# Splitting the third weight chunk of the two gated up projections earlier, and taking the last stage's mean of squares after two contraction tiles

## What is computed

```python
def rmsnorm(x, g):
    xf = x.astype(jnp.float32)
    y = xf * lax.rsqrt(jnp.mean(xf * xf, axis=-1, keepdims=True) + EPS)
    return (y * g.astype(jnp.float32)).astype(x.dtype)

def swiglu(x, w_gate, w_up, w_down):
    return (jax.nn.silu(x @ w_gate) * (x @ w_up)) @ w_down

h = h + 0.5 * swiglu(rmsnorm(h, ffn1_norm[l]), ffn1_w_gate[l], ffn1_w_up[l], ffn1_w_down[l])
...
h = h + 0.5 * swiglu(rmsnorm(h, ffn2_norm[l]), ffn2_w_gate[l], ffn2_w_up[l], ffn2_w_down[l])
```

## Time and profile before

| | |
|---|---|
| median of 3 runs | 2094.03 us |
| lowest, highest | 2090.93, 2095.31 us |
| the profiled execution's own time | 2093.15 us |
| its span, first to last instruction | 2091.3 us |
| PE busy | 1983.7 us (95%) |
| DVE busy | 1005.7 us (48%) |
| ACT busy | 727.0 us (35%) |
| mean granted TensorE clock | 0.983 |
| DMA, mean over the span | 93 GB/s |

### The profile page before, as it was taken

One profiled execution on the slowest core, in us unless ns is written; L12 is line 12 of the kernel. 1 busy time (PEld: TensorE's weight loads), 2 busy tenths in 40 slices (PEclk: granted clock), 3 DMA queues, 4 the chain that ended last, 5 costly groups with the idle time before them and its releaser, 6 DMA issues.

```text
span 2091.3 us, 26797 instructions
## 1 busy us (share of the span) xinstructions
PE 1983.7 (95%) x10909; PEld 1671.3 (80%) x10909; DVE 1005.7 (48%) x1364; ACT 727.0 (35%) x972; POOL 23.8 (1%) x45
## 2 busy tenths in 40 slices
PE   5899999997999999979999999899999999999997
PEld 2787887873888888769999999687888878888885
DVE  7688753436455542264443322667323454444323
ACT  2454444324445532152222212455333332222111
POOL 0100000000000000000000000000000000000000
PEclk9999999998999999999999999999999999999999
DMA  6644212220222222212222222211112222222221
GB/s 269 215 158 134 99 61 102 102 99 20 81 97 83 100 83 97 102 39 82 100 80 94 72 95 92 73 61 42 61 61 81 102 81 99 100 100 74 97 90 61
DMA packets 34847, 195.45 MB, mean 93 GB/s; under 512 B 3680, under 2 KB 3696, under 8 KB 19552
## 3 DMA queue, kind: packets, MB, share of 16 engines
q1 hardware_dynamic: 29008, 173.55, 23.6%
q0 software_dynamic: 5776, 21.02, 3.1%
HBM read 192.46 MB, written 2.10 MB: 93 GB/s over the span
## 4 chain that ended last, share of the span: by engine, by line
PE 88%; DVE 8%; ACT 2%; issue 1%; DMA 1%; SPq 0%; DVEq 0%; ACTq 0%
PE PS L600 86%; DVE W_lo L1625 2%; DVE INV L1669 1%; DMA A_low<-in_wada 1%; PE PS L756 1%; ACT W_hi L1184 1%; DVE N L1674 1%; DVE A_high L2103 1%; DMA ring<-in_wada 0%; DVE ring L2103 0%; DVE RS L1646 0%; DVE PT_lo L1707 0%; DVE stats L1692 0%; DVE X L2135 0%; DVE stats L1856 0%
## 5 line engine op out<-in xcount | busy, mean ns | idle before, releaser
L600 PE MATMUL PS<-H_hi,W_hi 128*128 128x512 f32 (+1 forms) x1976 | 632.2, 354 | 48.8 <-DVE H_lo L1657 19.4
L600 PE MATMUL PS<-H_hi,W_lo 128*128 128x512 f32 (+1 forms) x1976 | 632.9, 354 | 0.0
L600 PE MATMUL PS<-H_lo,W_hi 128*128 128x512 f32 (+1 forms) x1976 | 632.0, 354 | 0.0
L1625 DVE TENSOR_TENSOR W_lo<-W_raw,W_hi 128x2048 fp32r<-128x2048 f32 (+2 forms) x170 | 352.9, 2076 | 311.6 <-ACT W_hi L1184 311.0
L600 PEld LDWEIGHTS PS<-H_hi,W_hi 128*128 128x128 f32 x1976 | 350.0, 191 | 106.6 <-issue 42.8
L1184 ACT ACTIVATE W_hi<-W_raw 128x2048 fp32r<-128x2048 f32 (+2 forms) x170 | 295.6, 1739 | 325.4 <-PE PS L600 324.6
L600 PEld LDWEIGHTS PS<-H_lo,W_hi 128*128 128x128 f32 x1976 | 349.3, 191 | 50.6 <-issue 0.2
L600 PEld LDWEIGHTS PS<-H_hi,W_lo 128*128 128x128 f32 x1976 | 349.1, 191 | 49.9 <-issue 0.2
L600 PE MATMUL PS<-G_hi,W_lo 128*128 128x512 f32 (+1 forms) x704 | 210.2, 339 | 0.0
L600 PE MATMUL PS<-G_hi,W_hi 128*128 128x512 f32 (+1 forms) x704 | 209.6, 338 | 0.0
L600 PE MATMUL PS<-G_lo,W_hi 128*128 128x512 f32 (+1 forms) x704 | 209.3, 338 | 0.0
(11 more groups left out here) (246 smaller groups left out, 2045.2 us busy)
## 6 DMA issues: line engine op xcount, KB each, us to landing
W_raw<-in_wts SPq DMA_DIRECT2D x119, 1024.0 KB, 4.8
W_raw<-in_wdown SPq DMA_DIRECT2D x48, 704.0 KB, 4.1
ring<-in_wada POOLq DMA_DIRECT2D x32, 512.0 KB, 3.8
A_high<-in_wada SPq DMA_DIRECT2D x6, 1024.0 KB, 18.0
A_low<-in_wada SPq DMA_DIRECT2D x2, 1024.0 KB, 10.5
X<-in_xT SPq DMA_DIRECT2D x2, 1024.0 KB, 10.0
X<-in_xT POOLq DMA_DIRECT2D x1, 2048.0 KB, 8.8
out<-N SPq DMA_DIRECT2D x8, 256.0 KB, 2.1
```

The lines of the kernel that those rows point to most:

```text
L600: return nc.tensor.matmul(*a, **kw)
L1625: vector.tensor_tensor(W_lo[:, c.odd, 0:size], W_raw[:, c.odd, 0:size], W_hi[:, c.odd, 0:size].bitcast(FP32), ALU.subtract).then_inc(w_lo, 1)
```

## The change

`walk` no longer puts the third chunk's split between the first and the second chunk's products in the first round of a stage with `after_first`. `late_root` on ACT and DVE now has that split inside: on ACT between the last square and the square root, on DVE between the additions and the reciprocal. On PE, the mean of squares of `up3` is taken after 2 contraction tiles of the second chunk's first output tile in place of 6; in `up2` it stays after 6.

```diff
@@ walk
-                    if after_first is not None and step == 0 and k == 0:
-                        after_first()
                     body(i, step, k)
...
             if after_first is not None:
-                chunks_of_round(0, 0, s.words[0])
+                split(At(s.c + 1), s.words[0])
+                after_first()
+                for k in range(per):
+                    body(0, 0, k)
                 first = 1
@@ project, on PE
                     if m == 0 and within_first is not None:
-                        feature_tile(outs_of(b, m, tok, at), c.odd, 0, tiles * P, range(6), act_hi, act_lo, stop=False)
+                        n = 6 if tok == TOK else 2
+                        feature_tile(outs_of(b, m, tok, at), c.odd, 0, tiles * P, range(n), act_hi, act_lo, stop=False)
                         within_first()
-                        feature_tile(outs_of(b, m, tok, at), c.odd, 6 * tiles * P, tiles * P, range(6, KT), act_hi, act_lo, start=False)
+                        feature_tile(outs_of(b, m, tok, at), c.odd, n * tiles * P, tiles * P, range(n, KT), act_hi, act_lo, start=False)
                         continue
@@ up_second, on ACT
                 def root():
                     late_squares(n, squares_left)
+                    split(At(s.c + 2), WC)
                     late_root(n)
@@ late_root, on DVE
-            def late_root(n):
+            def late_root(n, between=lambda: None):
...
+                between()
                 dve.wait_ge(*n.reach("deviation", 1))
@@ up_second, on DVE
-                walk(dve, split, s, FH, 2, body, lambda: late_root(n))
+                walk(dve, split, s, FH, 2, body, lambda: late_root(n, lambda: split(At(s.c + 2), WC)))
```

## The result

| | before | with the change |
|---|---|---|
| median | 2093.36 us (4 runs) | 2082.11 us (4 runs) |
| lowest, highest | 2090.93, 2095.31 us | 2080.16, 2083.20 us |
| ratio, 95% interval | | 0.9946 (0.9933 to 0.9960) |
| profiled execution, own time | 2093.15 us | 2081.93 us |
| its span | 2091.3 us | 2079.2 us |

The change makes the kernel 11.3 us faster (0.54%). Measured again in two later groups of runs the changed kernel had 2081.17 and 2080.79 us against 2093.05 and 2094.10 us before. The forecast was 2081.4 us.

The account below looks back on a forecast made before the run. PE was taken to bound the kernel, busy 1983.7 of 2091.3 us. Stalls and clock, 3.83 + 3.98 + 1.64 + 2.75 = 12.20 us, off 2093.15 gave 2080.95; 2081.4 was taken, range 2078 to 2086.5.

Parts of the forecast that it names:

- The stalls: PE's waits ahead of the third chunk in `up2` and `up3` go whole: 3.83 and 3.98 us.
- The moved matmul at nothing: Earlier mean of squares in `up3` gains nothing; banks' spare time 2.8 us with it, 1.3 us without.
- The clock: 1.2 GHz stretches behind the stalls go: 1.64 us in `up2`, 2.75 in `up3`; bounds nothing to 5.5 us.
- One sign of being wrong: In the profile after, low-clock stretches on PE adding up to as much as before would show the forecast wrong.
- The first (the clock gives its part back): Rival: stalls go, but PE meets the same slow stretches elsewhere or another place slows; 2085.3 us; chance 0.10.
- The second: Rival: banks come late in one stage, at worst losing all of `up2`'s 5.47 us; 2086.4 us; chance 0.03.
- third: Rival: the stall moves to the fourth chunk, PE waiting as long 48 matmuls later; 2093 us; chance 0.03.
- The fourth: Rival: third chunk's raw weights late, holding back ACT's root, PE losing one for one; 2099 us at L = 13; chance 0.02.

Follow-up runs that it names:

- the kernel with `up2` alone: Kernel before with the third chunk's split moved in `up2` only, `up3` as before with its mean of squares after 6 tiles: 2087.78 us, ratio 0.9972.
- The experiment with the mean alone: Kernel before with only the mean of squares of `up3` taken after 2 tiles, both splits at their old places: 2087.88 us, ratio 0.9976.
- the experiment with the split ahead of the squares: Changed kernel with ACT's split one step further ahead, before the squares that are left: 2100.42 us, ratio 1.0035 to the kernel before.
- ACT alone: Changed kernel with DVE's low part of the third chunk's split back at its old place: 2085.18 us, ratio 0.9964 to the kernel before; again 2083.92 us.
- the mean at 6: Changed kernel with the mean of squares of `up3` left after 6 tiles: 2080.55 us, ratio 0.9939 to the kernel before; again 2080.95 us.

## Why the prediction was right

*The stalls.* Both went whole, as forecast: 3.83 and 3.98 us. Every step of the working can be laid beside its row. For `up2` the fair comparison is the kernel with `up2` alone, since its low stretch at the start of the stage is as long as before (2.9 against 3.0 us of busy PE). That stage began 0.74 us later than before (908.22 against 907.48), so 0.74 is to be added: `W_lo` at 924.89 (measured 924.80), the reciprocal at 927.58 (927.49), the third chunk at 933.94 (933.85). In the changed kernel's `up3` the second chunk began 5.4 us earlier than before, so 5.4 is to be taken off: `W_hi` at 1702.75 (1702.79), the root at 1705.9 (1706.02), the reciprocal at 1707.0 (1706.95), the banks free at 1711.8 (1711.62).

*An agreement that is luck.* In the changed kernel's profile `W_hi` of `up2` starts at 920.84 (forecast 920.83), the banks are free at 931.59 (931.65) and the third chunk starts at 933.15 (933.20). The stage began 1.35 us earlier than before, though, and the longer low stretch at its start (6.0 against 3.0 us of busy PE) cost PE 1.5 us. The two shifts cancel for what hangs on PE. `W_lo`, which hangs on the additions, started 1.35 us earlier than forecast, so its spare time ahead of the reciprocal was 1.7 us. In the kernel with `up2` alone it was as forecast: DVE was idle for 0.40 us between `W_lo` and the reciprocal (0.39 forecast).

*The moved matmul at nothing.* Shown beside the moved split: 2080.95 us without it and 2080.79 with it. Its spare times came out at 1.4 and 2.9 us (1.3 and 2.8).

*The clock.* The low stretches behind both stalls are gone, and the term was needed: the stalls alone (7.8 us) don't make the 11.3, 11.9 and 13.3 us of the three groups. Its size was one draw, though. The Trainium skill (TensorE: Matmul & The Clock Gate, "What's actually happening") says that the number of slow matmuls varies between runs, and the trace agrees: behind the stall of `up3` 5.8 us of busy PE ran at 1.2 GHz in both profiles of the kernel before, but 3.1 us in the kernel with `up2` alone, and the whole changed kernel had 34.1 to 46.6 us in three executions. The 2.75 us of the sum are thus the higher of the two values seen, about 2.8 and 1.5 us. The experiment with the mean alone shows how the term comes about: the stall fell from 3.8 to 1.1 us, the clock stayed at 1.00, and 5.5 us were saved.

One sign of being wrong that the prediction named needs more than one profile: low-clock stretches that add up to as much as before. In the first two profiles of the change they add up to 43.6 and 46.6 us, where 48.0 before less the 9.2 behind the two stalls would be 38.8. Over all five profiles with both splits moved and nothing else changed but the mean's place it is 40.2 on average, against 50.6 in the two before, so the stretches did not come back elsewhere. But the spread between executions of one program, 12.5 us, is larger than what the change took away, and one pair of profiles could not have told.

*A term that was missing.* Two chunks of `up2` take 23.50 us before and 23.36 us with the change, at a clock of 1.00 in both. Over the 10 rounds that follow, 0.14 us each, that is 1.4 us that no step of the prediction has. It is hidden in the sum because the change's profiled execution ran 3 us more of PE work at 1.2 GHz behind the norm ahead of `up2` than the one of before. From the first matmul of `up2` to the end of `down2` 394.17 us became 388.68 us, 5.5 saved as forecast, but out of 3.83 + 1.64 + 1.4 less 1.5 (5.4). With the pitch in it the sum would be 13.6 in place of 12.2, and the three groups measured 11.3, 11.9 and 13.3 us: that the median came within 0.7 us of the forecast is in part luck. Both kernels with one stage moved have the narrower pitch too, so their sum of 11.6 us holds it twice. That the pitch changed because of this edit isn't shown.

*The rivals.* The first (the clock gives its part back) fell: no low stretch stands in the 499 us piece, and none behind the first matmuls of `up2` in the 389 us piece. The second and third fell with the absence of any wait of PE in the stages. The fourth was priced right in kind: the experiment with the split ahead of the squares held the root back, and PE lost one for one, 5.4 and 5.1 us. Its total, 19.3 us over the change where 15 were expected, is 4 us more. The table gives 17 in the spans against the profile beside it, of which 4.5 are low clock (8.9 us more of it, halved) and 11.5 idle. That profile is the fastest of the five runs, 2.5 us under their median, and the rest of the difference isn't traced.

## What to carry to other kernels

A piece of work put ahead of a chain on an in-order engine is free as long as the chain itself is waiting for another engine there, or as long as what it holds back isn't wanted yet. `up2` is the first case. `up3` is the second: the split and the table load behind it held the root back by about 1 us (PE's mean ended at 1703.94 + 1.02 = 1704.96, and the root came at 1706.02), and the banks were free 2.9 us early all the same. So look for the idle row with a releaser, and put there what the bound engine needs next, on every engine that takes part. One place further ahead it holds the chain back, here at 19 us for one instruction's move on one engine in two stages. Price a stall of PE of some microseconds with the slow matmuls behind it, and one of about a microsecond without. In these profiles every stall of 3.7 to 5.4 us in `up2` and `up3` was followed by 3.1 to 5.8 us of busy PE at 1.2 GHz, none of the stalls of 1.1 and 0.6 us was, and the one of 2.4 us in the mixing layer was in six of 13 profiles. When two edits shorten the same wait, test them alone and together: the moved mean here is worth 5.5 us without the moved splits and nothing with them.

## What the runs showed of the hardware that was not expected

At a granted clock of 1.00 and without waits, PE's pitch in `up2` has two values. PE's window over 200 us of that stage, in the kernel with the mean at 2 alone:

```profile
950.00:1150.00 200.00, 200.00 (x1637) 1.00 0.24 88
```

In the kernel with the split moved in `up3` alone:

```profile
950.00:1150.00 200.00, 200.00 (x1646) 1.00 0.25 88
```

1637 matmuls against 1646 in the same time, 0.55%; the changed kernel has 1646 too. It stayed with the kernel where one was profiled again (before twice the slower, ACT alone twice the slower, the change three times the faster, the mean at 6 twice the faster). Of the kernels profiled once, the mean at 2 alone and the split ahead of the squares have the slower, the others the faster. Yet the change in `up3` alone and the mean at 2 alone have the same instructions in `up2` in the same order, and differ in it. What in the built program decides it was not tried.
